# Reordering weight splits against norm and sine work on ScalarE and VectorE in a two-block transformer kernel

## The chip, the cores and the metric

The kernel runs on one core of one Trainium2 chip. The metric is the device time of one execution in microseconds (us), lower is better. The core has five engines with in-order programs: TensorE (PE), VectorE (DVE), ScalarE (ACT), GpSimd (POOL) and SyncE (SP, which here only issues DMAs). They meet through semaphores.

## The reference

One input of 512 tokens by 1024 channels goes through two different transformer blocks in float32. The parts that matter here, cut:

```python
def first_block(x, ...):
    x = _layer_norm(x, ln_emb_g, ln_emb_b)
    proj = x @ w_in[l]                       # q_r, f_r, f_a, g_r, q_a, k_a, i_r, v_a
    o_a = _rms_norm_heads(_fox_attention(q_a, k_a, v_a, logf_a))
    o_r = _rms_norm_heads(_hgrn2_chunked(silu(q_r), k_r, i_r, logf_r)) * silu(g_r)
    mix = concatenate([o_a, o_r]) @ w_o[l]
    x = _layer_norm(ALPHA * x + mix, ln_mix_g, ln_mix_b)
    h = _causal_depthwise_conv(x @ w_up[l], conv_w, conv_b)
    a, u = split(h, 2)
    return _layer_norm(ALPHA * x + (gelu(a) * u) @ w_down[l], ln_ffn_g, ln_ffn_b)

def second_block(x, ...):   # neighbourhood attention, a Hyena mixer, SwiGLU
    # its Hyena filters depend on no token:
    hid = sin(fr * (z @ w1 + b1))
    hid = sin(fr * (hid @ w2 + b2))
    h = (hid @ w3).reshape(L, 2, HY_ORDER, HY_WIDTH) * decay
```

## The kernel before

**Three products for one.** Every float32 operand of a large matmul is split in two: a high part, which ACT writes (a Copy into a rounded format), and a low part, which DVE writes (source minus high part). PE then adds three products in PSUM (lines 540 to 542). A weight item is 128x2048. SP loads the items in the order of a plan into a ring of three `raw` buffers, and a buffer is loaded again when the low part of the item three places earlier is written. ACT's `high(upto)` (line 1140) writes `whi`, DVE's `low_parts(upto)` (line 1736) writes `wlo`; both go on, in order, up to the item named. They are called at chosen places of the ACT and DVE programs, which are written out by hand, one program per engine. There are two `whi`/`wlo` pairs for most items, so the item in a pair can be replaced when PE has used it.

**Token columns.** `channels(u)` stands in three programs. PE transposes 128 tokens in two halves (line 553); ACT scales the first half and DVE the second out of PSUM (four pieces each), ACT writes both high parts `xh`, DVE both low parts `xl`. Four such calls serve the first norm (u = 0 to 3) and four the second (u = 4 to 7).

**The start.** Items 0 and 1 (`J_QR`) give q_r. PE takes them in `two_pieces` (line 681): the first 256 tokens for the four output tiles, then the last 256 tokens for the same four. The first half needs the columns of u = 0 and 1, and item 0. Between these tiles PE also runs the two small matmuls of the sines of the Hyena filters, `sine(0)` after the third tile of the first half and `sine(1)` after the first tile of the second half. DVE turns each result into a sine argument in a chain of seven operations (lines 1797 to 1802), ACT takes the sine. Then PE goes on with item 2 (`J_FR`, the forget gate), the filter taps, and item 3. ACT's program at this place is

```python
            high(J_FR)
            ac.wait_ge(sig["sn_v"], 14)
            ac.wait_ge(sig["cst"], 4)
            act(h2[0:64, :], q4[2][0:64, :], ACT.Sin, "sn")
            act(h2[64:P, 0:1], q4[2][64:P, 0:1], ACT.Sin, "sn")
            for i in range(4):
                if i == 3:
                    high(J_FR + 1)
                silu_q(i)
```

where `sn_v` reaches 14 at the end of the second sine chain, and `silu_q(i)` empties tile i of q_r out of PSUM. `high(J_FR)` waits for PE to be through with item 0.

**PSUM banks.** `Fills.take` (line 73) hands out banks in turn within a named pool, and makes PE wait until the bank's last tile has been emptied:

```python
        b = POOLS[pool][self.turn[pool] % len(POOLS[pool])]
        self.turn[pool] += 1
        if self.emptied[b]:
            pe.wait_ge(*self.emptied[b])
```

The q_r tiles come from the pool "dense" (banks 0 to 4), the transposes and sines before them from "first" (banks 4 to 7). After them the pool is "all" (banks 0 to 7), whose turn begins at 0.

**The first FFN.** Items `J_UP` to `J_UP + 21` give 44 tiles of 128 channels. PE takes `J_UP` and `J_UP + 1` in `two_pieces`, and the others as pairs of 128x512 tiles. For each tile ACT copies it out of PSUM with the middle weight of the convolution (`scaled`), DVE adds the two neighbours (`neighbours`, line 2146, two operations), and ACT applies gelu to the first tiles of each group. At chosen places DVE also accumulates the second block's modulation (`ada`, lines 1861 and 1864), two 128x2048 operations per item. At the same time POOL applies the scale and shift of the norm to `X` (`affine`, line 2508, eight operations of 128x1024), which wait for the last transposes.

Of the kernel before, what the change touches and what calls it, by code (L numbers as in the profile page):

```python
# [110 lines left out]
def split_no(kind, i):  # L111
    return SPLITS[kind] + i + 1
# [77 lines left out]
J_QR, J_FR, J_F, J_GR, J_Q, J_K, J_IR, J_V = 0, 2, 4, 5, 7, 9, 11, 13  # L190
J_DFT, J_TAP, J_WO, J_UP, J_DOWN = 15, 16, 20, 24, 46
# [50 lines left out]
def used_by(j):  # L242

    return SHARED[SHARED.index(j) - 2]
# [16 lines left out]
def build(nc, ins, out):  # L261
    with ExitStack() as ctx:  # L262
# [15 lines left out]
        def flat(x):  # L278
            return x[:, :, :].rearrange("p a b -> p (a b)")
# [28 lines left out]
        def pcol(name, i=0, rows=P):  # L308
            a = PCOLS[name] + i
            return pc[0:rows, a:a + 1]  # L310

        def ln_cols(inst, t):
            a = 15 * (4 * inst + t)
            return small[:, a:a + 12], small[:, a + 12:a + 14], small[:, a + 14:a + 15]
# [175 lines left out]
        def parts_of(j):  # L490
            return ahead[j] if j in OWN else (whi[buffer_of(j)][:, :], wlo[buffer_of(j)][:, :])
# [12 lines left out]
        def ch_part(x, hf, t):  # L504

            if isinstance(x, list):
                return x[hf][t // 2][:, :, P * (t % 2):P * (t % 2) + P]
            return x[:, 4 * hf:4 * hf + 4, P * t:P * t + P]
# [6 lines left out]
        def ch_scale(u, k):  # L515
            if u < 8:
                return pcol("ln_emb_g" if u < 4 else "ln_mix_g", k)
            a = 56 if u < 10 else 48 if u < 14 else 40
            return mod[:, a + k:a + k + 1]

        def ch_bias(u, k):
            if u < 8:
                return pcol("ln_emb_b" if u < 4 else "ln_mix_b", k)
            a = 16 if u < 10 else 0 if u < 14 else 32
            return mod[:, a + k:a + k + 1]
# [589 lines left out]
        def ch_again(u, hf):  # L1115

            return 2 * (u - 2) + hf + 1 if u in (2, 3, 6, 7, 12, 13) else 2 * (u - 1) + hf + 1 if u == 9 else 0
# [9 lines left out]
        def scalar_program(eng):  # L1127
# [3 lines left out]
            def act(dst, src, func, signal=None, **more):  # L1131
                m = ac.e.activation(dst, src, func, **more)  # L1132
                if signal:
                    m.then_inc(sig[signal], 1)

            def tile(key):
                ac.wait_ge(sig["pe"], at[key])
                return bank[key]

            def high(upto):  # L1140

                while conv[0] <= min(upto, len(conv_at) - 1):
                    j = conv[0]
                    i = conv_at[j]
                    ac.wait_ge(raw_sem[i % 3], 16 * (i // 3 + 1))
                    if j == J_UP:
                        ac.wait_ge(sig["pe"], at["w", J_WO])
                    elif j == J_TAP:
                        ac.wait_ge(sig["h_ke"], 2)
                        ac.wait_ge(sig["h_qe"], 2)  # L1150
                    elif j in (J_TAP + 2, J_TAP + 3):
                        ac.wait_ge(sig["pe"], at["w", j - 2])
                    elif j == J_K2:
                        ac.wait_ge(sig["sp_lo"], split_no("down0", 7))
                    elif j == J_UP2:
                        ac.wait_ge(sig["pe"], at["w", J_MERGE + 3])
                    elif j in (J_DOWN2, J_DOWN2 + 1):
                        ac.wait_ge(sig["pe"], at["fast", N_FAST - 1, 4 if j > J_DOWN2 else 1])
                    elif j >= 2 and j != J_TAP + 1:
                        ac.wait_ge(sig["pe"], at["w", used_by(j)])  # L1160
                    if j == J_DFT2 + 2:
                        ac.wait_ge(sig["tab"], 4)
                    act(parts_of(j)[0], raw[i % 3][:, :], ACT.Copy, "whi")
                    conv[0] += 1
# [6 lines left out]
            def normal(inst, t):  # L1171
                _, mv, rs = ln_cols(inst, t)
                ac.wait_ge(sig["ln_nm"], 4 * inst + t + 1)
                act(X[:, t, :], X[:, t, :], ACT.Identity, "ln_x", bias=mv[:, 1:2], scale=rs)

            def channels(u):
                m = ch_tmp[u][0]
                ac.wait_ge(sig["ch_lo"], ch_again(u, 0))
                b = tile(("ch", u, 0))
                for q in range(4):  # L1180
                    c = slice(P * q, P * q + P)
                    act(m[:, c], b[:, c], ACT.Identity, "ch_a" if q == 3 else None, bias=ch_bias(u, q), scale=ch_scale(u, q))
                hi, _, t = ch_dst[u]
                for hf in range(2):
                    ac.wait_ge(sig["ch_v" if hf else "ch_a"], u + 1)
                    act(ch_part(hi, hf, t), ch_tmp[u][hf].rearrange("p (k c) -> p k c", k=4), ACT.Copy, "ch_hi")
# [22 lines left out]
            channels(0)  # L1209
            root(0, 3)  # L1210
            normal(0, 3)
            high(0)
            channels(1)
            channels(2)
            high(1)
            channels(3)
# [174 lines left out]
            normal(1, 3)  # L1391
            channels(6)
            channels(7)
            high(J_UP + 2)


            def scaled(v, key, y, name, n, w0, c):
# [324 lines left out]
        def vector_program(eng):  # L1722
# [3 lines left out]
            def up(m, signal):  # L1726
                m.then_inc(sig[signal], 1)
# [8 lines left out]
            def low_parts(upto):  # L1736

                while conv[0] <= min(upto, len(conv_at) - 1):
                    j = conv[0]
                    ve.wait_ge(sig["whi"], conv_no(j))  # L1740
                    hi, lo = parts_of(j)
                    up(ve.e.tensor_tensor(lo, raw[conv_at[j] % 3][:, :], hi.bitcast(F32), ALU.subtract), "wlo")  # L1742
                    conv[0] += 1
# [13 lines left out]
            def inverse(inst, t):  # L1757
                _, mv, rs = ln_cols(inst, t)
                ve.wait_ge(sig["ln_sd"], 4 * inst + t + 1)
                up(ve.e.reciprocal(rs, rs), "ln_rs")  # L1760
                ve.wait_ge(sig["ln_rs"], 4 * inst + t + 1)
                up(ve.e.tensor_scalar(mv[:, 1:2], mv[:, 0:1], rs, -1.0, ALU.mult, ALU.mult), "ln_nm")

            def channels(u):
                m = ch_tmp[u][1]
                ve.wait_ge(sig["ch_lo"], ch_again(u, 1))
                b = tile(("ch", u, 1))
                for q in range(4):
                    c = slice(P * q, P * q + P)
                    o = ve.e.tensor_scalar(m[:, c], b[:, c], ch_scale(u, 4 + q), ch_bias(u, 4 + q), ALU.mult, ALU.add)  # L1770
                up(o, "ch_v")
                hi, lo, t = ch_dst[u]
                for hf in range(2):
                    ve.wait_ge(sig["ch_hi"], 2 * u + hf + 1)
                    up(ve.e.tensor_tensor(ch_part(lo, hf, t), ch_tmp[u][hf].rearrange("p (k c) -> p k c", k=4),  # L1775
                                          ch_part(hi, hf, t).bitcast(F32), ALU.subtract), "ch_lo")
# [11 lines left out]
            def sine(i, rows, bias):  # L1788
                a, num = q4[2][0:rows, :], q4[1][0:rows, :]

                def step(k, m):
                    up(m, "sn_v")
                    ve.wait_ge(sig["sn_v"], 7 * i + k)
                b = tile(("sine", i))
                ve.wait_ge(sig["consts"], 32)
                ve.wait_ge(sig["sn"], i)
                step(1, ve.e.tensor_scalar(a, b[0:rows, :], bias, pcol("hy_freq", 0, rows), ALU.add, ALU.mult))
                step(2, ve.e.tensor_scalar(num, a, 1.0 / 6.283185307179586, MAGIC, ALU.mult, ALU.add))
                step(3, ve.e.tensor_scalar(num, num, MAGIC, None, ALU.subtract))
                for k, c in enumerate(TWO_PI):  # L1800
                    step(4 + k, ve.e.scalar_tensor_tensor(out=a, in0=num, scalar=-c, in1=a, op0=ALU.mult, op1=ALU.add))
                step(7, ve.e.tensor_scalar(a, a, PI, -PI, ALU.min, ALU.max))
# [12 lines left out]
            inverse(0, 2)  # L1815
            channels(0)
            inverse(0, 3)
            low_parts(0)
            channels(1)
            channels(2)  # L1820
            low_parts(1)
            channels(3)
# [3 lines left out]
            up(ve.e.tensor_tensor(flat(wsum)[0:64, 0:1024], wf, wb, ALU.add), "cst")  # L1826
            up(ve.e.tensor_tensor(flat(wsum)[0:64, 1024:2048], wf, wb, ALU.subtract), "cst")
            up(ve.e.tensor_scalar(flat(wsum)[64:P, 0:1024], flat(wsum)[64:P, 1024:2048], -1.0, None, ALU.mult), "cst")
            sine(1, P, pcol("hy_b2"))
            low_parts(J_FR)  # L1830
            low_parts(J_FR + 1)

            def taps(n, t):
# [301 lines left out]
            low_parts(J_UP + 1)  # L2135
            channels(6)
            channels(7)
            low_parts(J_UP + 2)


            def neighbours(v, key, y, name, n, steps, c):
# [874 lines left out]
```

## Time and profile before

| | |
|---|---|
| time, median of 3 runs | 1708.51 us (1707.31 to 1710.93) |
| the profiled execution | 1708.51 us, span 1706.7 us |
| PE matmul busy | 1595.5 us, 93% of the span |
| PE weight load busy | 1335.1 us, 78% |
| DVE busy | 1056.9 us, 62% |
| ACT busy | 700.4 us, 41% |
| POOL busy | 439.5 us, 26% |
| mean granted clock of PE | 0.976 |

The span runs from the first to the last instruction of the profiled execution; the time holds 1.8 us around it. An engine's busy time overlaps with that of the others. A busy PE says that matmuls were in flight, and a gap in it is time in which it waited for another engine. The granted clock is 1.00 at 2.4 GHz and 0.50 at 1.2 GHz. Averages over the span say little here, since the change touches two short stretches; these are read from the timeline.

### The profile page before, as it was taken

The page shows a single profiled execution, that of the slowest core. Times are in us where ns is not written, and L with a number is a line of the kernel's source. Part 1 is how long each engine was busy: PE and PEld are TensorE (multiplying, and loading weights), DVE is VectorE, ACT ScalarE, POOL GpSimd, SP SyncE. Part 2 cuts the span into 40 slices and gives each one's busy share as a digit, 9 for nine tenths or more (in the row PEclk, how much of TensorE's full clock was granted, in tenths as well). Part 3 has the DMA queues.
Part 4 walks back from the last instruction along what each step waited for, and adds up shares of the span by engine and source line. Part 5 has one row for each costly group of instructions (what it writes and reads, how often), then busy time and mean ns, then how long its engine had stood idle before and what let it go on. Part 6 is the DMA issues. An engine that isn't in the chain of part 4 may idle for free. (4 is left out here: it accounts for less than half of the span.)

```text
span 1706.7 us, 21205 instructions
## 1 busy us (share of the span) xinstructions
PE 1595.5 (93%) x8576; PEld 1335.1 (78%) x8576; DVE 1056.9 (62%) x1458; ACT 700.4 (41%) x1021; POOL 439.5 (26%) x360
## 2 busy tenths in 40 slices
PE   5999988988999999999799999998899899998996
PEld 5778875766878888788788778887787899998885
DVE  6675547447987486433765543346853699998333
ACT  5644245543533243323632334444444544443222
POOL 0023303320622011100052012223432655553002
PEclk8999999989999899999899999999999999999998
DMA  7242212342254254222426423224443132224211
GB/s 285 99 148 75 75 62 89 118 176 99 99 173 164 107 197 173 99 99 74 147 99 248 130 76 109 85 84 152 151 166 124 38 112 99 99 100 148 76 73 50
DMA packets 46924, 203.93 MB, mean 119 GB/s; under 512 B 14337, under 2 KB 14721, under 8 KB 28203
## 3 DMA queue, kind: packets, MB, share of 16 engines
q1 hardware_dynamic: 37202, 171.84, 28.1%
q0 software_dynamic: 9088, 30.38, 5.3%
q8 instruction: 68, 1.11, 0.3%
q10 hardware_dynamic: 536, 0.35, 0.1%
q14 instruction: 30, 0.24, 0.0%
HBM read 181.56 MB, written 21.00 MB: 119 GB/s over the span
## 5 line engine op out<-in xcount | busy, mean ns | idle before, releaser
L540 PE MATMUL ps<-xh,whi 128*128 128x512 f32 (+1 forms) x1096 | 395.5, 361 | 10.8 <-DVE wlo L1742 5.3
L542 PE MATMUL ps<-xh,wlo 128*128 128x512 f32 (+1 forms) x1096 | 390.0, 356 | 0.0
L541 PE MATMUL ps<-xl,whi 128*128 128x512 f32 (+1 forms) x1096 | 388.2, 354 | 0.0
L1742 DVE TENSOR_TENSOR wlo<-raw,whi 128x2048 fp32r<-128x2048 f32 x93 | 233.3, 2509 | 138.3 <-ACT whi L1132 138.3
L1132 ACT ACTIVATE whi<-raw 128x2048 fp32r<-128x2048 f32 (+1 forms) x173 | 221.9, 1310 | 137.8 <-PE ps L542 52.1
L540 PEld LDWEIGHTS ps<-xh,whi 128*128 128x128 f32 x1096 | 208.8, 190 | 53.0 <-issue 11.6
L541 PEld LDWEIGHTS ps<-xl,whi 128*128 128x128 f32 x1096 | 209.2, 191 | 29.3
L542 PEld LDWEIGHTS ps<-xh,wlo 128*128 128x128 f32 x1096 | 207.9, 190 | 31.0
L540 PE MATMUL ps<-whi,xh 128*128 128x512 f32 x304 | 122.9, 404 | 8.3 <-ACT vr L1132 3.7
L542 PE MATMUL ps<-whi,xl 128*128 128x512 f32 x304 | 121.8, 401 | 0.0
L541 PE MATMUL ps<-wlo,xh 128*128 128x512 f32 x304 | 121.6, 400 | 0.0
L2146 DVE SCALAR_TENSOR_TENSOR xr<-ps,pc,xr 128x511 f32<-128x511 f32 x88 | 65.2, 747 | 44.7 <-ACT xr L1132 43.2
L2508 POOL TENSOR_TENSOR act<-xr 128x512 f32<-128x512 f32 x22 | 39.1, 1781 | 203.0 <-DVE xr L2146 202.6
L2434 DVE TENSOR_TENSOR wlo<-raw,whi 128x512 fp32r<-128x512 f32 x80 | 82.7, 1062 | 0.0
L540 PEld LDWEIGHTS ps<-whi,xh 128*128 128x128 f32 x304 | 58.1, 191 | 24.5 <-issue 8.6
L1132 ACT ACTIVATE xr<-ps,pc 128x512 f32<-128x512 f32 x44 | 33.9, 773 | 101.0 <-PE ps L542 101.0
L540 PE MATMUL ps<-whi,ah 128*128 128x512 f32 x176 | 69.8, 397 | 3.1 <-issue 3.1
L541 PE MATMUL ps<-wlo,ah 128*128 128x512 f32 x176 | 69.8, 396 | 0.0
L542 PE MATMUL ps<-whi,al 128*128 128x512 f32 x176 | 69.8, 396 | 0.0
L542 PEld LDWEIGHTS ps<-whi,xl 128*128 128x128 f32 x304 | 57.9, 190 | 14.2
L541 PEld LDWEIGHTS ps<-wlo,xh 128*128 128x128 f32 x304 | 58.0, 191 | 13.9 <-issue 0.2
L1132 ACT ACTIVATE xr<-xr 128x512 f32<-128x512 f32 (+1 forms) x32 | 24.5, 767 | 107.0 <-DVE xr L2146 62.8
(449 smaller groups left out, 3358.2 us busy)
## 6 DMA issues: line engine op xcount, KB each, us to landing
raw<-in_w_in SPq DMA_DIRECT2D x35, 1024.0 KB, 5.1
raw<-in_ffn_w SPq DMA_DIRECT2D x33, 1024.0 KB, 4.8
raw<-in_ada SPq DMA_DIRECT2D x24, 1024.0 KB, 4.8
raw<-in_w_up SPq DMA_DIRECT2D x22, 1024.0 KB, 4.8
raw<-in_w_down SPq DMA_DIRECT2D x11, 1024.0 KB, 4.8
xd<-X POOLq DMA_DIRECT2D x8, 512.0 KB, 6.1
td<-vr POOLq DMA_DIRECT2D x16, 256.0 KB, 3.6
raw<-td SPq DMA_DIRECT2D x4, 1024.0 KB, 5.3
```

Source lines behind the costliest of these rows:

```text
L540: pe.e.matmul(o, lh, rh, start=start, stop=False)
L541: pe.e.matmul(o, lh, rl, start=False, stop=False)
L542: return pe.e.matmul(o, ll, rh, start=False, stop=stop)
L1132: m = ac.e.activation(dst, src, func, **more)
L1742: up(ve.e.tensor_tensor(lo, raw[conv_at[j] % 3][:, :], hi.bitcast(F32), ALU.subtract), "wlo")
L2146: up(ve.e.scalar_tensor_tensor(out=y[:, o], in0=b[:, i], scalar=pcol(name + "_w", n * w + c), in1=y[:, o], op0=ALU.mult, op1=ALU.add), "cv ...
L2434: up(ve.e.tensor_tensor(lo, product_source(n, p), hi.bitcast(F32), ALU.subtract), "wlo")
L2508: po.e.tensor_tensor(dst, a, b, op).then_inc(sig[signal], 1)
```

## The change

Calls are moved in the ACT and DVE programs; no instruction is added or removed.

- At the start, `channels(1)` comes before the split of item 0, on ACT (`high(0)`) and on DVE (`low_parts(0)`).
- On DVE, the low part of item 2, `low_parts(J_FR)`, comes before the second sine chain, `sine(1)`.
- Ahead of the first FFN's loop, `high(J_UP + 2)` and `low_parts(J_UP + 2)` are taken out. The loop splits this item itself: its second turn calls `high(J_UP + 2)` and `low_parts(J_UP + 2)`, after the work on tiles 0 and 1.

```diff
@@ scalar_program
             normal(0, 3)
+            channels(1)
             high(0)
-            channels(1)
             channels(2)
@@
             channels(6)
             channels(7)
-            high(J_UP + 2)
@@ vector_program
             inverse(0, 3)
+            channels(1)
             low_parts(0)
-            channels(1)
             channels(2)
@@
             up(ve.e.tensor_scalar(flat(wsum)[64:P, 0:1024], flat(wsum)[64:P, 1024:2048], -1.0, None, ALU.mult), "cst")
+            low_parts(J_FR)
             sine(1, P, pcol("hy_b2"))
-            low_parts(J_FR)
             low_parts(J_FR + 1)
@@
             channels(6)
             channels(7)
-            low_parts(J_UP + 2)
```

## Rows read from the trace of the kernel before

**Rows 1.** Windows: length, busy PE, PEld, DVE, ACT, POOL, PE clock, DMA share, GB/s.

```profile
52.90:212.90 160.00, 158.91 (x762) 125.20 (x760) 94.27 (x121) 70.63 (x72) 45.31 (x44) 1.00 0.30 105
212.90:427.40 214.50, 185.66 (x934) 142.45 (x933) 121.67 (x274) 98.38 (x187) 42.49 (x49) 0.96 0.31 108
478.00:697.00 219.00, 218.84 (x964) 177.11 (x964) 151.94 (x132) 74.65 (x83) 34.59 (x20) 0.98 0.44 159
```

**Rows 2.** Timeline, start: start us, us, engine, line, operation [idle before <-releaser].

```profile
18.21 1.89 ACT L1132 ACTIVATE whi<-raw 128x2048 fp32r<-128x2048 f32 x1
20.01 1.48 ACT L1132 ACTIVATE tmp<-ps,pc 128x128 f32<-128x128 f32 x4
20.14 2.29 DVE L1742 TENSOR_TENSOR wlo<-raw,whi 128x2048 fp32r<-128x2048 f32 x1 [3.11 <-ACT whi L1132]
21.52 0.63 ACT L1132 ACTIVATE xh<-tmp 128x512 fp32r<-128x512 f32 x1
23.62 1.47 DVE L1775 TENSOR_TENSOR xl<-tmp,xh 128x512 fp32r<-128x512 f32 x2
25.24 0.55 PE L540 MATMUL ps<-xh,whi 128*128 128x256 f32 x1 [0.36 <-DVE xl L1775]
```

**Rows 3.** Timeline around the second sine: DVE, then ACT, then PE.

```profile
44.77 0.81 DVE L1797 TENSOR_SCALAR vr<-ps,pc 128x512 f32<-128x512 f32 x1
...
48.72 0.43 DVE L1802 TENSOR_SCALAR vr<-vr 128x512 f32<-128x512 f32 x1
49.42 2.29 DVE L1742 TENSOR_TENSOR wlo<-raw,whi 128x2048 fp32r<-128x2048 f32 x1 [0.27 <-ACT whi L1132]
...
47.40 1.92 ACT L1132 ACTIVATE whi<-raw 128x2048 fp32r<-128x2048 f32 x1 [5.15 <-PE ps L542]
49.22 0.84 ACT L1132 ACTIVATE gr<-vr 64x512 f32<-64x512 f32 x2
50.07 1.28 ACT L1132 ACT_TABLE_LOAD   x1
51.37 1.58 ACT L1132 ACTIVATE qr<-ps 128x512 f32<-128x512 f32 x3
...
52.90 0.39 PE L540 MATMUL ps<-xh,whi 128*128 128x512 f32 x1
```

**Rows 4.** Timeline of PE: two restarts after a wait.

```profile
216.72 0.47 PE L540 MATMUL ps<-whi,xh 128*128 128x512 f32 x1 [3.72 <-ACT vr L1132]
...
849.05 0.55 PE L540 MATMUL ps<-xh,qnr 128*128 128x256 f32 x1 [5.63 <-DVE xl L1775]
```

**Rows 5.** Windows behind three restarts of PE (columns of rows 1).

```profile
25.24:30.00 4.76, 4.76 (x22) 4.76 (x23) 3.57 (x7) 4.73 (x9) 0.00 (x0) 0.50 1.02 418
217.80:221.20 3.40, 3.40 (x10) 2.62 (x9) 1.39 (x3) 0.00 (x0) 0.00 (x0) 0.50 0.84 275
849.05:852.70 3.65, 3.65 (x17) 3.65 (x18) 1.65 (x5) 3.62 (x8) 0.00 (x0) 0.51 0.00 0
```

**Rows 6.** Timeline at the start of the first FFN: POOL, then DVE, then PE.

```profile
434.38 24.51 POOL L2508 TENSOR_TENSOR X<-X,bc 128x1024 f32<-128x1024 f32 x8 [60.49 <-PE ps L553]
...
440.58 4.48 DVE L1742 TENSOR_TENSOR wlo<-raw,whi 128x2048 fp32r<-128x2048 f32 x1
447.88 1.53 DVE L2146 SCALAR_TENSOR_TENSOR xr<-ps,pc,xr 128x511 f32<-128x511 f32 x2 [1.37 <-ACT xr L1132]
449.33 1.45 DVE L1861 TENSOR_SCALAR ch<-raw,cs 128x2048 f32<-128x2048 f32 x1
450.70 3.43 DVE L1861 TENSOR_SCALAR cl<-raw,cs 128x2048 f32<-128x2048 f32 x1
475.81 2.29 DVE L1742 TENSOR_TENSOR wlo<-raw,whi 128x2048 fp32r<-128x2048 f32 x1 [2.50 <-ACT whi L1132]
...
464.49 0.50 PE L540 MATMUL ps<-xh,whi 128*128 128x512 f32 x1 [0.81 <-DVE wlo L1742]
...
478.16 0.50 PE L540 MATMUL ps<-xh,whi 128*128 128x512 f32 x1 [2.20 <-DVE wlo L1742]
```

## The prediction

> **What bounds the kernel now.** I read the busy shares first, then windows over the stretches behind each moved call, to learn whether a delay there can be given back. PE is busy in 158.91 of the 160.00 us that follow its start on item 2, and in 218.84 of 219.00 us in the first FFN from 478 us on [rows 1]. In both stretches the order of PE's own work sets the end, and what PE loses ahead of them stays lost. Only from 212.9 to 427.4 us does it wait more, 28.8 us in all [rows 1]. Then I read the timeline at the three places, asking of each PE instruction which of its conditions came last: the low part of a weight, the low part of the columns, or a free bank.
>
> **Part 1: `channels(1)` ahead of item 0.** Before, ACT splits item 0 from 18.21 to 20.10 and then does the columns; DVE follows, and PE starts at 25.24, released by the columns' low part `xl` (end 23.62 + 1.47 = 25.09) [rows 2]. The other order takes the same pieces. From 18.21 ACT does 1.48 us of scaling and two high parts of 0.63 us (to about 20.9), then the 1.89 us of item 0 (to 22.8); DVE's own half of the columns lies beside that, and its 2.29 us low part of item 0 ends at about 25.1 [rows 2]. PE now waits for `wlo` instead of `xl` and starts at about 25.2 to 25.3. One releaser takes the place of the other, so the price is 0.1 us at most; I take 0.1, with -0.3 (the 0.36 us of waiting in that row) and +0.5 as bounds. The transposes of u = 3, which wait for these columns to leave their banks, come earlier but are not last. The load of item 3, issued when `wlo` of item 0 is written, comes 2.7 us later (25.1 against 20.14 + 2.29); its high part stands behind three Silu operations that end at 51.37 + 1.58 = 52.95 [rows 3], so this is covered.
>
> **Part 2: the low part of item 2 ahead of the second sine.** The low part waits for the high part, and ACT writes that from 47.40 to 49.32, since it must wait for PE to leave item 0. DVE does the sine chain from 44.77 to 49.15 while it would be idle, and the low part starts at 49.42, 0.27 us after the chain, released by ACT [rows 3]. It can't come sooner in the new order. So the move gains nothing on item 2, and PE did not wait there either: it passes to item 2 at 52.90 without idle time [rows 3].
>
> What is queued behind the waiting instruction is the point. DVE now stands idle from about 44.8 to 49.4, writes the low part to 51.7, and runs the 4.38 us of the sine (44.77 to 49.15) after it, to 56.0. ACT's two sines come behind the chain in order, and behind them its Silu of the q_r tiles: from the start of the sines to the start of the Silu 51.37 - 49.22 = 2.15 us, and 1.58 / 3 = 0.53 us for the first tile [rows 3]. Now 56.05 + 2.15 + 0.53 = 58.7 us, plus about 0.1 us for the signal, so 58.8.
>
> Who waits for the Silu? PE's first tile of item 2. The q_r tiles hold banks 0 to 3; the pool that follows begins its turn at bank 0, so that tile needs bank 0, and that is free when q_r tile 0 has been emptied. Before, this was at 51.37 + 0.53 = 51.9, a full 1.0 us ahead of PE. Now PE waits from 52.9 to 58.8: 5.9 us. The gate chain on ACT and DVE begins with that tile and shifts with it, so no engine keeps a lead.
>
> PE's clock adds to this. After waits of 3.72 and 5.63 us PE ran at half clock (1.2 GHz) for 3.40 and 3.65 us of its work, and at the start of the kernel for 4.76 us [rows 4, 5]. Half of that is lost, 1.7 to 2.4 us. I take 2.1, with 0 as the lower bound. Part 2 costs 5.9 + 2.1 = 8.0 us, with 5.5 and 8.5 as bounds.
>
> The page "ScalarE: Activation LUTs" of the Trainium skill, section "What ACT_TABLE_LOAD costs", counts 2.66 us for a switch of the function set, load and drain together. The row shows a load of 1.28 us and the Silu starting directly behind it, so I use the row; by the page the sum would be 1.4 us larger, which is no end of my range.
>
> **Part 3: item `J_UP + 2` split inside the loop.** Before, its low part runs from 440.58 to 445.06, before the first `neighbours`, at a time when PE is still in `two_pieces` [rows 6]. Afterwards it stands behind tiles 0 and 1. `neighbours` of tile 1 ends at 447.88 + 1.53 = 449.4 (up to 0.3 us sooner, since DVE is free earlier). Behind it ACT does the gelu and then the high part. The same sequence later in the loop leaves DVE idle for 2.50 us before the low part [rows 6], so this one starts at about 451.8. It takes 2.29 us when undisturbed and took 4.48 us beside POOL's `affine` work, which fills 434.38 to 458.89 [rows 6]; I take 3.4 us, so 455.2. PE wants the item when `two_pieces` ends. The item after it took 478.16 - 2.20 - 464.49 = 11.5 us of PE's time, so before, this one ran from 464.49 - 0.81 - 11.5 = 452.2 [rows 6]. That is a new wait of about 3.0 us.
>
> What follows is DVE's. `ada`, before at 449.33 to 454.1, comes behind the low part. Its two operations took 1.45 and 3.43 us, the second beside POOL; I take 3.9 for both, since POOL has had DVE's idle time to move ahead. So `ada` ends at 459.1 instead of 454.1. Of the 5.0 us about 1 comes back in the next operations, which before still ran beside `affine`, and 4.0 us stay. That PE lives from DVE here is seen before too: it waits 0.81 us for `wlo` at 464.49 and 2.20 us at 478.16, and from then on hardly at all [rows 1, 6]. So PE's start at 478.16 moves by what DVE is late: 4.0 us. As bounds, 0.5 us (low part 2.29, `ada` 2.9, all the contention gone) and 7 us (4.48 and 4.88, and none of it given back).
>
> The page "SBUF — State Buffer" of the Trainium skill, section "SBUF: two separate sides", says that DVE operations with two SBUF inputs and GpSimd operations take one port pair in turn, each for its whole instruction. The two durations of the low part agree with that. By that rule alone POOL's eight operations are a fixed amount that idle time of DVE lets through, which is the reason for the lower bound and for the third rival.
>
> **Sum.** The profiled execution took 1708.51 us, which is also the median. 1708.5 + 0.1 + 8.0 + 4.0 = 1720.6 us.
>
> **Rivals.**
> - *The clock is kept over the new wait before item 2.* For it: behind the wait of 2.20 us at 478.16 the clock was 0.98 in the mean of the stretch [rows 1, 6]. Against: 5.9 us is longer than both waits of [rows 4]. It takes 2.1 away: 1718.5 us.
> - *PE doesn't need bank 0.* Then item 2 starts at 52.90 and the late sine is first wanted by the filter taps behind item 2, at 52.9 + 11.5 = 64.4 us, long after 57. Only part 3 is left: 1712.6 us. Against it is the order in which the pools are handed out; for it only that no row of before shows PE waiting there.
> - *POOL's work takes the idle time of DVE.* Then the contention ahead of 464 us is used up in the gaps that the change makes, part 3 is at its lower bound of 0.5, and the sum is 1717.1 us. For it: nearly 2.2 us of the old low part is contention. Against: `affine` still fills the time until about 456.
> - *The early delay is swallowed: not slower.* Between 212.9 and 427.4 PE waits 28.8 us in all. If the releasers there ran to a time of their own (a load, or a chain that began before 53 us), the 8.0 us would vanish in these waits; with part 3 it decides at 3.4 us, below which the result is within 0.2%: 1709 to 1712.6 us. Against: the rows name ACT and DVE as releasers [rows 4], whose work there begins with the gate tile that is itself late.
> - *The clock also falls in the first FFN,* after one of its three waits of 2 to 3 us, and DVE is at its upper bound: 1725 us.
>
> **How the numbers follow.** My forecast, 1720.6, has a chance of 0.52. Clock kept 0.13; bank not needed 0.05; POOL's work in the idle time 0.14; swallowed 0.06; clock falls twice 0.10. The range 1714 to 1725 takes in the forecast, the first and the third rival and most of the last, and leaves out about 0.15. A measurement of this kernel tells about 0.2% (3.4 us) from no change. Slower by more is every case but the swallowed one and a part of the bank's: 0.92. Within 0.2%: 0.06. Faster: 0.02, for an error that I don't see.
>
> **What would show it.** Part 1: PE's first product within 0.5 us of 25.24, released by `wlo`. Part 2: the low part of item 2 still at 49.4, the sine chain from 51.6, the first Silu at about 58.2, and a wait of PE of 5.9 us before item 2 with ACT's `qr` as its releaser; a half clock for 3 to 5 us of the work after it. Window 52.9 to 212.9 moved as a whole. Part 3: the low part of `J_UP + 2` at about 452, a PE wait of 2 to 4 us before that item, and the product that stood at 478.16 later by 12 us, 8 from part 2 and 4 from here. Wrong would be: no wait before item 2 (the bank), or a shift that shrinks between 213 and 427 us (swallowed), or a shift in the first FFN under 1 us.

## The result, and the profile after

The changed kernel takes 1721.35 us (median of 4 runs, 1720.35 to 1725.12) against 1708.64 us before (4 runs, 1707.31 to 1710.93): 12.7 us more, a ratio of 1.0085 with a 95% interval of 1.0068 to 1.0100. The forecast was 1720.6 us with a range of 1714 to 1725. The profiled execution took 1722.57 us, its span 1720.7 us. It and four more executions of the changed kernel, 1722.57 to 1725.96 us, have none of the kernel before at their side and are not in the ratio; they allow a cost nearer to 14 us.

The start of the changed kernel, from its timeline (start us, us, engine, line, operation, in brackets the idle time before and who ended it); these lines answer to [rows 2]:

```profile
18.14 1.48 ACT L1132 ACTIVATE tmp<-ps,pc 128x128 f32<-128x128 f32 x4
19.66 1.15 ACT L1132 ACTIVATE xh<-tmp 128x512 fp32r<-128x512 f32 x2
20.71 1.90 ACT L1132 ACTIVATE whi<-raw 128x2048 fp32r<-128x2048 f32 x1
...
22.64 2.29 DVE L1741 TENSOR_TENSOR wlo<-raw,whi 128x2048 fp32r<-128x2048 f32 x1 [1.03 <-ACT whi L1132]
```

The low part now ends at 24.93, and PE starts at 24.99 instead of 25.24, released by `wlo` instead of `xl`. The pieces are the same, and only the one that comes last has changed.

Around the second sine, DVE, then ACT, then PE; these answer to [rows 3]:

```profile
49.43 2.29 DVE L1741 TENSOR_TENSOR wlo<-raw,whi 128x2048 fp32r<-128x2048 f32 x1 [4.60 <-ACT whi L1132]
51.64 0.80 DVE L1796 TENSOR_SCALAR vr<-ps,pc 128x512 f32<-128x512 f32 x1
...
55.58 0.43 DVE L1801 TENSOR_SCALAR vr<-vr 128x512 f32<-128x512 f32 x1
...
47.48 1.92 ACT L1132 ACTIVATE whi<-raw 128x2048 fp32r<-128x2048 f32 x1 [5.15 <-PE ps L542]
56.04 0.85 ACT L1132 ACTIVATE gr<-vr 64x512 f32<-64x512 f32 x2 [6.64 <-DVE vr L1801]
56.91 1.28 ACT L1132 ACT_TABLE_LOAD   x1
58.21 1.57 ACT L1132 ACTIVATE qr<-ps 128x512 f32<-128x512 f32 x3
...
58.95 0.76 PE L540 MATMUL ps<-xh,whi 128*128 128x512 f32 x1 [5.80 <-ACT qr L1132]
```

The low part of item 2 stands where it stood (49.43 against 49.42). In front of it DVE is idle for 4.60 us, the time in which it used to do the sine. PE waits 5.80 us, and the releaser is ACT's `qr`, the Silu that empties a bank. That this wait is one for a bank, and that the bank is the link between a sine of the Hyena filters and the forget gate, is not in the line; an experiment below tests it.

Windows behind that wait, columns as in [rows 1]; the first two are to be held against [rows 5]:

```profile
59.00:63.60 4.60, 4.60 (x11) 3.63 (x12) 1.78 (x1) 3.28 (x5) 0.00 (x0) 0.50 0.00 0
58.95:64.60 5.65, 5.65 (x13) 4.42 (x14) 2.29 (x1) 3.33 (x5) 0.00 (x0) 0.50 0.00 0
59.00:221.50 162.50, 161.43 (x760) 127.09 (x760) 94.24 (x121) 71.36 (x73) 45.31 (x44) 0.98 0.28 98
221.50:438.40 216.90, 188.28 (x934) 144.76 (x933) 121.70 (x274) 98.43 (x187) 42.50 (x49) 0.94 0.31 107
```

PE runs at half clock (1.2 GHz) from its start on item 2 to about 64.6 us, 5.65 us. The stretch that took 160.0 us before, between the start on item 2 and the wait in front of item `J_V`, now takes 162.5 us. The one behind it takes 216.9 instead of 214.5 us, at a mean clock of 0.94 instead of 0.96 [rows 1]. Its waits are the same ones: 216.9 - 188.3 = 28.6 us, before 214.5 - 185.7 = 28.8 us.

The start of the first FFN, POOL, DVE and PE; these answer to [rows 6]:

```profile
445.42 22.61 POOL L2506 TENSOR_TENSOR X<-X,bc 128x1024 f32<-128x1024 f32 x8 [61.17 <-PE ps L553]
...
458.64 1.53 DVE L2144 SCALAR_TENSOR_TENSOR xr<-ps,pc,xr 128x511 f32<-128x511 f32 x2 [1.37 <-ACT xr L1132]
462.68 3.10 DVE L1741 TENSOR_TENSOR wlo<-raw,whi 128x2048 fp32r<-128x2048 f32 x1 [2.51 <-ACT whi L1132]
465.71 3.42 DVE L1860 TENSOR_SCALAR ch<-raw,cs 128x2048 f32<-128x2048 f32 x1
469.05 1.27 DVE L1860 TENSOR_SCALAR cl<-raw,cs 128x2048 f32<-128x2048 f32 x1
...
475.30 0.75 DVE L2161 TENSOR_SCALAR cx<-cx,small 128x1024 f32<-128x1024 f32 x1
475.97 2.28 DVE L1741 TENSOR_TENSOR wlo<-raw,whi 128x2048 fp32r<-128x2048 f32 x1
...
465.84 0.50 PE L540 MATMUL ps<-xh,whi 128*128 128x512 f32 x1 [2.33 <-DVE wlo L1741]
478.31 0.50 PE L540 MATMUL ps<-xh,whi 128*128 128x512 f32 x1 [1.00 <-DVE wlo L1741]
491.97 0.50 PE L540 MATMUL ps<-xh,whi 128*128 128x512 f32 x1 [2.20 <-DVE wlo L1741]
```

The three PE lines are its starts on `J_UP + 2`, `J_UP + 3` and `J_UP + 4`, behind waits of 2.33, 1.00 and 2.20 us; before, there was no wait at the first, and 0.81 and 2.20 us at the others [rows 6]. In the 4 us behind each of the three starts the granted clock is 1.00, so the rival in which it falls here too is out. The start of the FFN at 427.36 has moved to 438.41, by 11.05 us, and the start of `J_UP + 4` from 478.16 to 491.97, by 13.81 us. So part 3 costs 2.76 us in the trace. The same starts, read along the kernel, say where the whole comes from:

| PE's start on | before | after | later by |
|---|---|---|---|
| first product | 25.24 | 24.99 | -0.25 |
| item 2 | 52.90 | 58.95 | 6.05 |
| item `J_V` | 216.72 | 225.35 | 8.63 |
| item `J_WO` | 370.27 | 380.64 | 10.37 |
| item `J_UP` | 427.36 | 438.41 | 11.05 |
| item `J_UP + 4` | 478.16 | 491.97 | 13.81 |
| `down` of the first FFN | 700.44 | 712.68 | 12.24 |
| end of the span | 1706.7 | 1720.7 | 14.0 |

### The profile page after: what moved, and what is told of

It is laid out like the page before. It is cut to its first block and busy times, and to the rows that moved or that the text cites. A ratio compares the mean times of both kernels' runs of the same rounds, so it can differ in the third digit from the quotient of the medians.

```text
span 1720.7 us, 21205 instructions
## 1 busy us (share of the span) xinstructions
PE 1600.4 (93%) x8576; PEld 1338.8 (78%) x8576; DVE 1053.0 (61%) x1458; ACT 700.5 (41%) x1021; POOL 436.9 (25%) x360
## 3 DMA queue, kind: packets, MB, share of 16 engines
q8 instruction: 68, 1.11, 0.3%
## 5 line engine op out<-in xcount | busy, mean ns | idle before, releaser
L540 PEld LDWEIGHTS ps<-xh,whi 128*128 128x128 f32 x1096 | 209.2, 191 | 64.6 <-issue 16.9
```

What stands on the lines that cost most here:

```text
L540: pe.e.matmul(o, lh, rh, start=start, stop=False)
```

## The experiments

Each kernel is the kernel before with the edit named, unless another is named. The ratio is that of a kernel's runs to runs of the kernel before on the same chips; their median was 1709.56 us for the four runs that split the change, and 1710.44 us for the others. Traces start at slightly different offsets (25.12 to 25.34 for the first product), which I subtract where a few tenths matter.

**The three parts one by one.** Part 1 alone:

```diff
-            high(0)
-            channels(1)
+            channels(1)
+            high(0)
```

with the same on DVE.

> Part 1 alone: channels(1) ahead of item 0's split on ACT and DVE, all else as before. Theory (one releaser takes the other's place): PE's first product within 0.5 us of 25.24, now released by wlo; the time within 0.2% of before. Rival (the three parts act together, and part 1 carries part of the 12.7 us of the whole change): at least 2 us slower.

It gave 1710.09 us, a ratio of 0.9999 (0.9990 to 1.0007). Its PE start, from the timeline:

```profile
25.12 0.58 PE L540 MATMUL ps<-xh,whi 128*128 128x256 f32 x1 [3.28 <-DVE wlo L1742]
```

Part 1 is nothing, by time (1.7 us less to 1.2 us more) and by trace. The releaser has changed from `xl` to `wlo`, and the idle time that now stands in one piece (3.28 us) was before cut up by transposes that can be done earlier.

Part 2 alone:

```diff
-            sine(1, P, pcol("hy_b2"))
-            low_parts(J_FR)
+            low_parts(J_FR)
+            sine(1, P, pcol("hy_b2"))
```

> Part 2 alone: the low part of item 2 ahead of the second sine on DVE. Theory (the sine's delay passes through ACT's Silu to bank 0 and to PE): a PE wait of 5.8 us before item 2 at about 58.9, half clock behind it, and 8.0 to 8.7 us more than before in all. Rival (the early delay is given back in the 28.8 us of PE waits between 213 and 427 us): the same wait, but under 3 us in the whole time.

It gave 1718.08 us, a ratio of 1.0046 (1.0034 to 1.0058), that is 7.9 us (5.8 to 9.9). PE's start on item 2:

```profile
58.85 0.77 PE L540 MATMUL ps<-xh,whi 128*128 128x512 f32 x1 [5.80 <-ACT qr L1132]
```

It waits 5.80 us, released by `qr`, as in the whole change; the product that stood at 216.72 comes at 225.07. Nothing is given back between 213 and 427 us, so the rival of the swallowed delay falls.

Part 3 alone:

```diff
-            high(J_UP + 2)
...
-            low_parts(J_UP + 2)
```

> Part 3 alone: item J_UP + 2 split inside the loop. Theory (DVE's chain is the bound up to the product that stood at 478.16, and is late by what the profile of the changed kernel shows): that product later by 2.8 us, and the whole 2.8 us more. Rival (PE's clock or the DVE margin behind it takes more of it back): under 1 us more. Rival (my forecast's size): 4.0 us more.

It gave 1713.96 us, a ratio of 1.0026 (1.0015 to 1.0036), that is 4.4 us (2.6 to 6.2). The two PE starts from its timeline:

```profile
456.52 0.50 PE L540 MATMUL ps<-xh,whi 128*128 128x512 f32 x1 [2.33 <-DVE wlo L1741]
...
469.00 0.50 PE L540 MATMUL ps<-xh,whi 128*128 128x512 f32 x1 [1.01 <-DVE wlo L1741]
```

They are the waits of the whole change to 0.01 us. From the start of `J_UP` (429.09) to that of `J_UP + 4` (482.67) it took 53.58 us, before 478.16 - 427.36 = 50.80 us: 2.78 us. The time's interval holds both that and my 4.0 us, so for the size only the traces tell them apart. It excludes the rival under 1 us. The parts add up: 0.9999, 1.0046 and 1.0026 make 1.0071, inside the interval of the whole.

**Is it the bank?** The pool after the q_r tiles is begun at another bank, once without and once with part 2:

```diff
             use[0] = "all"
+            fills.turn["all"] = 4
```

> The kernel before, with the pool of all banks begun at bank 4 instead of bank 0 once the q_r tiles are handed out. It is the control of the next run. Theory: PE did not wait for a bank at item 2, so item 2 starts at 52.9 as before and the time is within 0.3% of 1708.6; later tiles stand in other banks, which can move waits between 213 and 427 us by 1 to 2 us either way.

> Part 2 alone with the same rotation: item 2's first tile gets bank 4, which sine 0 has left long before. Theory (the bank that holds q_r tile 0 carries the stall): no wait before item 2, which starts at 52.9 with the sine as late as before (chain from 51.6). The gate chain on DVE is then late for another reason, the low part of item 3, which stands ahead of it and comes behind ACT's Silus at about 62 to 64 us, so a wait of up to 2 us behind the taps is possible; the whole is 0 to 4 us over the rotated control. Rival (PE waits for something else of ACT's, not the bank): the 5.8 us wait stays and the time is 8 us over the control.

The control gave 1712.28 us, a ratio of 1.0019 (1.0010 to 1.0027): the rotation itself brings a new wait of 6.17 us at 89.31, released by DVE's operation on a filter tap (line 1841), since the product there needs the bank that the tap holds. With part 2 it was 1717.66 us, 1.0054 (1.0035 to 1.0072). In the trace of that one, the passage to item 2 and the ACT line which ended PE's wait in the changed kernel:

```profile
52.85 0.28 PE L542 MATMUL ps<-xh,wlo 128*128 128x256 f32 x1
52.97 0.40 PE L540 MATMUL ps<-xh,whi 128*128 128x512 f32 x1
...
58.20 1.58 ACT L1133 ACTIVATE qr<-ps 128x512 f32<-128x512 f32 x3
```

The Silu is as late as in the changed kernel (58.20), and PE starts on item 2 at 52.97 with no wait. So the bank of q_r tile 0 carried the stall. My expectation was 0 to 4 us over the control. 1.0054 - 1.0019 is 0.35%, about 6 us, but the two intervals allow anything from about 2.6 to 9.5 us, and in the two traces the product of item `J_V` is 4.15 us later (228.72 against 224.57). So most of the price is still there, and whether it is over 4 us is open. DVE's lines say what it consists of, and the last one is PE's:

```profile
61.82 2.29 DVE L1743 TENSOR_TENSOR wlo<-raw,whi 128x2048 fp32r<-128x2048 f32 x1 [5.82 <-ACT whi L1133]
64.03 0.68 DVE L1902 TENSOR_SCALAR tmp<-ps 128x512 f32<-128x512 f32 x1
...
94.38 0.77 PE L540 MATMUL ps<-xh,whi 128*128 128x512 f32 x1 [11.40 <-DVE vr L1841]
```

The low part of item 3 waits for ACT's high part, which stands behind the late Silus, and DVE's work on the gate tile (line 1902) stands behind that low part. That work starts at 64.03, in the control at 58.94: 5.1 us later. PE meets the delay at the product that needs the tap's bank, where its wait is 11.40 instead of 6.17 us. With these banks, the free bank moves the stall to a later tile that DVE has to empty and does not remove it. But the control waits at that place already, so the delay passes on in full there; how much of it would reach PE if bank 0 alone were free, no run shows.

**Is the rest of part 2 the clock?** Part 2, with 25 extra products in PE's wait, into a bank whose content is not read afterwards:

```diff
             use[0] = "all"
+            pe.wait_ge(sig["sn_v"], 1)
+            for _ in range(25):
+                pe.e.matmul(fills.banks[4][:, :], xh1[:, 0, 0:P], xh1[:, 0, :], start=True, stop=True)
```

> Part 2 alone, and in PE's wait before item 2 another 25 products of 128x512 of the token columns are computed into bank 4, whose content nothing reads afterwards; this is extra work, the output is the reference's. They take about 25 x 0.233 = 5.8 us and stand just where PE waits. Theory (2.7 us of the 8.7 us in the trace is half clock behind the wait): the clock stays at 1.00, item 2 starts at about 59.0 as in the run without them, and the whole costs 6.0 us instead of 8.7. Rival (the clock is no part of it, the rest is another wait): as slow as part 2 alone.

It gave 1716.24 us, a ratio of 1.0026 (1.0015 to 1.0037), against 1.0046 without the extra work; the difference is 0.20%, about 0.16% either way. Windows over the extra products, and behind the start of item 2:

```profile
52.70:58.70 6.00, 5.93 (x27) 4.58 (x26) 2.93 (x5) 2.81 (x5) 0.00 (x0) 1.00 0.42 165
58.70:62.00 3.30, 3.26 (x14) 2.69 (x15) 0.38 (x1) 3.27 (x5) 0.00 (x0) 1.00 0.00 0
```

and the same place in part 2 alone:

```profile
59.00:63.30 4.30, 4.30 (x11) 3.34 (x12) 1.58 (x1) 3.18 (x5) 0.00 (x0) 0.50 0.00 0
```

Item 2 starts at 58.74 and at 58.85, so the wait has been filled and not shortened. The product that stood at 216.72 comes at 222.59 instead of 225.07, 2.5 us sooner, with the clock at 1.00. Against the kernel before it is 5.8 us later, counted from the first product: the wait alone. Useless work in the wait makes the kernel faster, and the clock is what differs between the two traces. This half clock is what remained of part 2's cost once the 5.8 us of the wait are taken off.

**What sets the price of part 3?** POOL's scale and shift operations are moved from in front of the FFN's loop into its turns 2 to 5, without and with part 3:

```diff
-            for t in range(4):
-                affine(t)
             for j2 in range(11):
...
+                if 2 <= j2 <= 5:
+                    affine(j2 - 2)
```

> The kernel before, with POOL's eight scale and shift operations spread over turns 2 to 5 of the first FFN's loop instead of ahead of it. Theory (between 436 and 464 us DVE's operations with SBUF inputs lost 7 to 9 us beside them): the low part at 440.58 takes 2.3 instead of 4.5 us, ada about 2.9 instead of 4.9, and the PE waits of 0.73, 0.81 and 2.20 us vanish: 3 us faster, 1705.5. Behind 490 us DVE has a lead and the contention costs nothing. Rival (the durations are DVE's own or come from a DMA): the same durations and the same time.

> Part 3, with POOL's scale and shift operations moved out of the way as in affine_later. With the contention gone the old low part would cost 2.3 us of an idle DVE, and the new place leaves a PE wait: neighbours to 449.6, 2.5 us for gelu and high part, 2.3 us for the low part, so 454.3 against 451.9 where PE wants it. Theory: a PE wait of 2.4 us before item J_UP + 2, none before J_UP + 3, 0.5 us before J_UP + 4, so 2.5 us over affine_later (1706.5), about 1709. Rival (the cost of part 3 was the contention itself): as fast as affine_later.

Without part 3 it gave 1706.52 us, a ratio of 0.9979 (0.9970 to 0.9987), faster than the kernel before by about 3.6 us. Its DVE lines:

```profile
440.29 2.29 DVE L1742 TENSOR_TENSOR wlo<-raw,whi 128x2048 fp32r<-128x2048 f32 x1 [1.11 <-ACT whi L1132]
...
449.53 1.28 DVE L1861 TENSOR_SCALAR ch<-raw,cs 128x2048 f32<-128x2048 f32 x1
450.72 1.28 DVE L1861 TENSOR_SCALAR cl<-raw,cs 128x2048 f32<-128x2048 f32 x1
```

The low part takes 2.29 instead of 4.48 us, and the two `ada` operations 1.28 each instead of 1.45 and 3.43 [rows 6]. Of the PE waits of 0.73, 0.81 and 2.20 us only 0.35 us is left. With part 3 on top it gave 1711.55 us, 1.0004 (0.9996 to 1.0013), so part 3 costs 0.25% here as it does without the move. The waits in front of `J_UP + 2` and `+ 4` are 1.50 and 1.32 us, and from `J_UP` to `J_UP + 4` it takes 49.60 us (429.18 to 478.78) against 46.85 us (428.85 to 475.70): 2.75 us. The contention is worth 3.6 us to the kernel, but taking it away leaves part 3 as dear as it was, 2.8 us. The parts of that price are not the same, though. `ada` ends about 5 us late in both cases (5.1 and 4.8 us, counted from the start of `J_UP`), and about 2 us of it comes back: with the contention because the later operations no longer run beside POOL, without it because DVE had idle gaps there (0.42, 1.11, 0.41 and 0.86 us in `affine_later`) that the delay fills.

Then the other condition in front of each low part, ACT's high part behind a gelu, is put ahead of it, without and with part 3:

```diff
                         if part == 0:
+                            if m:
+                                high(J_UP + 2 * j2 + 2)
                             ac.wait_ge(sig["cv_2"], v + 1)
```

> The kernel before, with ACT's high part of the next item put ahead of the second gelu of each group in the first FFN instead of behind it. Theory (DVE idles 2.5 us for that high part while DVE's chain is the bound up to 478.16): DVE's low part starts at about 473.4 instead of 475.81, the PE wait of 2.20 us at 478.16 goes, and the time falls by about 2 us to 1706.5. Rival (a later gelu or the buffer's last use holds it up): no change.

> Part 3, with ACT's high part of the next item ahead of the second gelu of each group, as in high_before_gelu. Theory (the 2.5 us for which DVE waits on ACT before each low part are the price of the new place): the low part of J_UP + 2 starts at about 449.6 instead of 451.8 (both counted from a start of item J_UP at 427.4), the PE waits before J_UP + 2, + 3 and + 4 fall from 2.33, 1.01 and 2.20 us to about 0.8, 0 to 0.5 and 0, and the time is 2 to 4 us under part 3 alone. Rival (the wait on ACT hides in DVE's chain): under 1 us gained.

The first gave 1709.94 us, 0.9999 (0.9990 to 1.0007). In its trace the wait of 2.20 us is gone, and from `J_UP + 3` to `down` it takes 698.90 - 465.16 = 233.7 us instead of 700.44 - 464.49 = 236.0. The next stretch, from `down` to the first transposes of the second block, takes 128.6 instead of 127.0 us in that execution. The time shows no gain, and I can't say that this one stretch is the reason. With part 3 it gave 1713.32 us, 1.0016 (1.0007 to 1.0025), against 1.0026 for part 3 alone; the intervals overlap. The wait in front of `J_UP + 2` (2.33 us) is gone too, but the one in front of `J_UP + 3` is 3.16 instead of 1.01 us. The difference of 0.10%, 1.7 us, is within the noise, so neither the expected 2 to 4 us nor nothing is shown. The trace shows why it is little up to `J_UP + 3`. The low part of `J_UP + 2` starts 2.2 us sooner (451.14 against 453.36), but behind it both `ada` operations run beside POOL, 3.42 and 3.43 us, where the second took 1.27 us in part 3 alone. The low part of `J_UP + 3` then starts only 0.2 us sooner, and PE, which has started earlier, waits longer for it. Each of the two edits removes one condition; no run removes both together under part 3, so that the rest of its price is the low part's new place in DVE's chain is read from the rows and not tested by itself.

**Both edits that are not part of the change:**

> The kernel before with both edits that are not part of the change: POOL's scale and shift operations later, and the high part ahead of the second gelu. In affine_later only 0.35 us of PE waits are left between 429 and 698 us. Theory: 0.35 us at most over affine_later, so the same time within the measurement, about 0.2% under before. Rival (each removes its own 2 to 3 us): 0.3% or more under before.

It gave 1709.34 us, 0.9989 (0.9980 to 0.9998), so 0.11% under the kernel before, where about 0.2% was expected. No PE wait over 0.3 us is left from 430 to 696 us, and still it is not below `affine_later` alone; as expected, the two edits do not add up, since they remove the same waits; the difference between these two kernels is within the noise. The fastest kernel of this study is the one with POOL's operations later.

## Why the prediction was right

**Part 1.** The new releaser and the sum over the pieces were right. It was put at 0.1 us; the trace of the whole gives -0.25 us, the time nothing.

**Part 2, the wait.** Right step by step: the low part of item 2 unmoved at 49.4, the sine chain from 51.64 (51.6 forecast), the Silu at 58.21 (58.2), a wait of 5.80 us (5.9) with `qr` as its releaser. That the q_r bank is the link was argued from the order of the banks, and is now shown by the rotation. One sentence was too simple: without the bank only part 3 would be left. DVE's work on the gate tile comes 5.1 us late behind the low part of item 3, a second path that the prediction did not have; with the rotated banks it costs 4 to 6 us.

**Part 2, the clock.** Put at 2.1 us. The shift grows from 6.05 us at item 2 to 8.63 at 216.72, so 2.6 us, and the filler gives 2.5 us. Right in kind, and half a us small: the half clock lasted 5.65 us (5.35 us in part 2 alone), where the three rows had 3.40 to 4.76 us. 8.0 us was forecast for the part, 8.9 and 8.3 came in the two traces (the shift at 216.72, less that of the first product), and 7.9 in the time.

On the function set, the 2.66 us of the page "ScalarE: Activation LUTs" of the Trainium skill, section "What ACT_TABLE_LOAD costs", would by estimate have had PE wait 1.4 us longer. The load takes 1.28 us again and the Silu follows directly, so the measurement decides for the row.

**Part 3.** The mechanism was right: a wait of 2 to 3 us in front of `J_UP + 2` (3.0 forecast, 2.33 measured) and DVE's chain as the bound to `J_UP + 4`. The size of the term was off, 4.0 us against 2.75 to 2.78 in three traces. The mis-sized piece is what comes back: `ada` ended 5.1 us late, counted from the start of `J_UP` (5.0 forecast). That this fits so well is partly luck: the low part took 3.10 us where 3.4 was taken, and `ada` 4.6 us where 3.9 was taken. The operations behind it, the low part of `J_UP + 3` included, gave back about 2.4 us, not 1. That low part took 2.28 instead of 3.38 us and the last `cx` 0.75 instead of 1.59, since POOL was through by then: its eight `affine` operations needed 22.61 us instead of 24.51, and its next two ended at 474.64. This is the third rival's mechanism, at part of its strength.

**The sum.** 0.1 + 8.0 + 4.0 = 12.1 us, measured 12.7 us in the medians and 14.0 us between the two profiled spans. That the sum is so near is luck in part: part 3 was put 1.2 us too high and the clock half a us too low, and something that stands in no term came on top. In the spans the three terms measure -0.25 + 8.9 + 2.8 = 11.4 us. The other 2.6 us come between 216.72 and 427.36, where the shift grows by 2.4 us with the same waits and a lower mean clock, and go partly back and forth later. I had not counted that in any term. It is not shown to belong to the change: the trace of part 1 alone is also 2.1 us later at `J_UP` (429.30 against 427.36, its first product 0.12 us earlier), and its time is that of the kernel before. In all seven traces whose work up to there is that of the kernel before (in one of them with part 1), `J_UP` starts at 428.03 to 429.40, so the profiled execution of the kernel before is the earliest. Its granted clock from 359 to 370 us is 1.00, and 0.71 to 0.86 in those seven.

## What to carry to other kernels

Moving an instruction ahead of other work gains nothing if its own input isn't there yet; the work that it displaces loses the idle time that hid it. Follow the delayed result through every in-order program and every buffer that is handed out in turn, here from a filter's sine through a Silu to a PSUM bank of an unrelated matmul, and count the clock's half speed behind a new wait of PE, here one of 5.80 us. Where two engines lengthen each other's instructions in a stretch that bounds the kernel, look whether the one with slack can do its work elsewhere: here moving POOL's operations gained 3.6 us, and none of the tested orders of DVE's or ACT's work gained anything clear of noise.

## What the runs showed of the hardware

- Extra products in a wait of PE made the whole faster: 1.0026 with them, 1.0046 without. With them the granted clock stayed at 1.00, where it was 0.51 in the mean of the first 5.35 us behind the wait.
- DVE operations beside POOL's took up to twice their time and more: 4.48 against 2.29 us for a subtraction of 128x2048, and 3.43 against 1.28 us for a product of a tensor with a column, which reads one tensor only. In the other direction, POOL's pairs of 128x1024 operations took 4.79 to 8.89 us beside a busy DVE in `affine_later`. No row has such a pair undisturbed. The page "SBUF — State Buffer" of the Trainium skill (section "SBUF: two separate sides") has DVE share a port pair with GpSimd both in operations with two SBUF inputs and in a two-port performance mode. The DVE durations agree with that, if the product with a column runs in such a mode, which no row here says.
- Single traces of kernels with the same waits differ by 1.5 to 3 us in stretches such as 480 to 700 us (222.3 us before, 220.7 after, 223.8 in part 2 alone), through the granted clock alone as far as the waits show. The start differs too: from 25.3 to 30 us the clock is 0.50 or 0.51 in the traces before, after and of part 2 alone, and 1.00 in those of part 1 and part 3 alone, where PE reaches item 2 at 52.0 to 52.1 instead of 52.90 us. Up to there part 3 alone is the same program as the kernel before, so the half clock behind the first product comes in some executions and not in others. A part of under 2 us is to be read between two near starts in the trace, not from the end of the span.
